# The middle tap of Hyena's short convolutions on ScalarE, and ScalarE's order in the attention piece by piece

## What is computed

```python
def centred_conv(u, w):
    k = w.shape[0]
    r = k // 2
    length = u.shape[1]
    up = jnp.pad(u, ((0, 0), (r, r), (0, 0)))
    out = up[:, 0:length] * w[0]
    for i in range(1, k):
        out = out + up[:, i:i + length] * w[i]
    return out

def hyena_branch(pp, conv_w, w1, b1, freq, w2, b2, w3, bias):
    ...
    u = centred_conv(pp[..., OFF_HY:OFF_FN], conv_w).astype(F32)
    parts = jnp.split(u, HY_ORDER + 1, axis=-1)
    ...

def diff_softmax(q, k, v, lam):
    s = jnp.einsum('bhqcd,bhkcd->bhcqk', q.astype(F32), k.astype(F32)) * (A_DQK ** -0.5)
    p = jax.nn.softmax(s, axis=-1)
    a = p[:, :, 0] - lam * p[:, :, 1]
    return jnp.einsum('bhqk,bhkv->bhqv', a, v.astype(F32))
```

## Time and profile before

| | |
|---|---|
| median of 3 runs | 2013.67 us (2009.11 to 2014.9) |
| the profiled execution's own time | 2014.24 us |
| its span in the profile | 2012.5 us |
| TensorE busy (matmul) | 1890.2 us, 94% |
| VectorE, ScalarE, GpSimd busy | 1142.8, 782.0, 603.4 us |
| TensorE's granted clock, mean | 0.978 of full speed |
| attention stage, layer 0 | about 409 to 560 us of the span, turns 442.6 to 551 |
| attention stage, layer 1 | about 1521 to 1606 us of the span, turns 1547 to 1600 |

### The profile page before, as it was taken

The page is one execution under the profiler, slowest core; times in us unless marked ns, Lnnn a source line. Parts: engine busy times, 40 slices in busy tenths (PEclk is TensorE's granted clock), DMA queues, the critical chain, the costliest instruction groups (busy, mean ns, idle before and its releaser), DMA issues.

```text
span 2012.5 us, 32086 instructions
## 1 busy us (share of the span) xinstructions
PE 1890.2 (94%) x11466; PEld 1540.3 (77%) x11466; DVE 1142.8 (57%) x2009; ACT 782.0 (39%) x1593; POOL 603.4 (30%) x537
## 2 busy tenths in 40 slices
PE   6999889989989999998999999999988899998999
PEld 2566667766658888876888888777776789998999
DVE  4745863766674333345443343359777665567575
ACT  2325531335524322333322232256534544445453
POOL 3333122552121212126220132443446431134020
PEclk8999889999999999999999999999999999999999
DMA  7344454346521323322323332222213235554554
GB/s 240 124 136 147 158 169 131 121 131 210 177 72 50 98 94 94 99 89 84 94 94 97 102 94 94 79 84 83 87 43 121 77 120 179 174 166 150 179 181 143
DMA packets 225007, 244.62 MB, mean 122 GB/s; under 512 B 11459, under 2 KB 213508, under 8 KB 223876
## 3 DMA queue, kind: packets, MB, share of 16 engines
q1 hardware_dynamic: 221168, 226.62, 36.2%
q10 hardware_dynamic: 3732, 16.60, 2.2%
HBM read 236.90 MB, written 6.29 MB: 121 GB/s over the span
## 4 chain that ended last, share of the span: by engine, by line
PE 68%; DVE 12%; issue 10%; POOL 4%; ACT 3%; DMA 3%; ACTq 0%; DVEq 0%; POOLq 0%; SPq 0%
PE psum L638 54%; PE psum L633 12%; DVE big L2449 3%; DMA raw<-in_w_ada_dram 2%; POOL whl L1496 2%; DVE big L2458 1%; POOL big L3385 1%; ACT big L1707 1%; ACT whl L1487 1%; POOL big L3256 1%; DVE rstd L2449 1%; ACT big L1704 1%; PE psum L746 1%; DVE big L2711 1%; DMA big<-in_hy_table_dram 0%
## 5 line engine op out<-in xcount | busy, mean ns | idle before, releaser
L638 PE MATMUL psum<-hhl,whl 128*128 128x512 f32 (+1 forms) x4416 | 829.8, 348 | 27.9 <-DVE hhl L2583 16.8
L638 PEld LDWEIGHTS psum<-hhl,whl 128*128 128x128 f32 x4416 | 702.1, 193 | 153.8 <-issue 42.7
L1487 ACT CAST whl<-raw 128x512 fp32r<-128x512 f32 x656 | 374.2, 618 | 859.7 <-PE psum L638 856.1
L1496 DVE TENSOR_TENSOR whl<-raw,whl 128x512 fp32r<-128x512 f32 x480 | 330.1, 729 | 484.3 <-ACT whl L1487 483.4
L638 PE MATMUL psum<-bigr,whl 128*128 128x512 f32 (+1 forms) x2688 | 469.9, 336 | 4.7 <-DVEq L3175 2.5
L638 PEld LDWEIGHTS psum<-bigr,whl 128*128 128x128 f32 x2688 | 414.4, 190 | 57.7 <-issue 4.7
L1496 POOL TENSOR_TENSOR whl<-raw,whl 128x512 fp32r<-128x512 f32 x176 | 235.1, 1357 | 455.9 <-ACT whl L1487 440.1
L633 PE MATMUL psum<-big 128*128 128x128 f32 (+8 forms) x1572 | 244.5, 330 | 22.3 <-DMA big<-in_hy_w_dram 5.0
L633 PEld LDWEIGHTS psum<-big 128*128 128x128 f32 (+4 forms) x1572 | 165.7, 179 | 81.8 <-issue 53.3
L638 PE MATMUL psum<-whl,hhl 128*128 128x512 f32 x672 | 165.3, 405 | 6.0 <-POOL whl L1496 4.7
L3385 POOL TENSOR_TENSOR big<-big,tmp 128x512 f32<-128x512 f32 (+1 forms) x64 | 64.5, 1020 | 339.2 <-DVE tmp L3172 338.2
(11 more groups left out here) (176 smaller groups left out, 1405.5 us busy)
## 6 DMA issues: line engine op xcount, KB each, us to landing
raw<-in_w_mlp_dram SPq DMA_DIRECT2D x128, 512.0 KB, 3.6
raw<-in_w_ada_dram SPq DMA_DIRECT2D x96, 512.0 KB, 5.2
raw<-in_w_in_dram SPq DMA_DIRECT2D x88, 512.0 KB, 3.7
raw<-in_w_gate_dram SPq DMA_DIRECT2D x64, 512.0 KB, 3.5
raw<-in_w_branch_dram SPq DMA_DIRECT2D x32, 512.0 KB, 3.5
raw<-in_w_o_dram SPq DMA_DIRECT2D x16, 512.0 KB, 3.5
hy_spectra<-big ACTq DMA_DIRECT2D x2, 2560.0 KB, 10.2
big<-hy_spectra ACTq DMA_DIRECT2D x2, 1280.0 KB, 5.6
```

Of the source, the lines that this page charges most:

```text
L638: m = nc.tensor.matmul(o_, a(p_), b(q_), start=first and i == 0, stop=last and i == 2, skip_group_check=shared)
L1487: nc.scalar.copy(whl[:, r, 0, ks], raw_of(n)[:, ks]).then_inc(S["hi_ready"], 1)
L1496: ins = eng.tensor_tensor(whl[:, r, 1, ks], raw_of(n)[:, ks], whl[:, r, 0, ks].bitcast(F32), ALU.subtract)
```

## The change

A semaphore `hy_begun` is added. ScalarE gets `hy_begin`: it waits for the block and for the turning of the block two before, and writes the block times the middle tap into `HYB["cb"]` as an Identity activation with a column of `cols` as scale; it does not wait for itself afterwards. `conv` leaves the multiply out for Hyena's blocks and waits for `hy_begun` instead, before its first addition; DeltaNet's keep it. `u_copies` goes away: for each piece of a slot ScalarE now does the cast, then for a whole block the u copy of the block two before and the begin of this one, before it comes to the next piece. TensorE's, GpSimd's and SP's programs are the same.

```diff
@@ -2199,13 +2199,11 @@
                     for s, kh, cb in slot:
                         if cb:
                             hi_ahead(act, hy_strip[li, s, kh])
-
-                def u_copies(slot):
-                    for s, kh, cb in slot:
-                        if kh and s:
-                            u_copy(li, 2 * s + cb - 2)
+                        if kh:
+                            if s:
+                                u_copy(li, 2 * s + cb - 2)
+                            hy_begin(li, 2 * s + cb)
                 hy_ahead(slots[0])
-                u_copies(slots[0])
...
                     hy_ahead(slots[1 + u])
-                    u_copies(slots[1 + u])
                     if li == 0:
                         mod_row(0, FIRST_MODS + u)
...
+            def hy_begin(li, blk):
+                act.wait_ge(unit_done, hy_mark[li, blk])
+                if blk >= 2:
+                    act.wait_ge(filled, fill_at["hyu", li, blk - 2] + 1)
+                tk = toks(li)
+                f(HYB["cb"][:, blk % 2, tk], unit_bank[hy_unit[li, blk] % UNITS][:, tk], ACT.Identity,
+                  scale=cols[:, li, 0, 76 + blk:77 + blk]).then_inc(S["hy_begun"], 1)
...
@@ -2628,7 +2633,10 @@
-                ts(d3, p3, w[1], None, MUL)
+                if key == "hy":
+                    dve.wait_ge(S["hy_begun"], 12 * li + blk + 1)
+                else:
+                    ts(d3, p3, w[1], None, MUL)
```

More of the change, by code:

```diff
@@ L379, in build @@
                  "gates_turned fn_odd mod_turned amp_ready inverse_ready "
-                 "g_split k_sums kr_ready scales_ready far_ready decay_ready A_ready dit_ready it_ready diag_copied solved u_cleared udiag_dve "
+                 "hy_begun g_split k_sums kr_ready scales_ready far_ready decay_ready A_ready dit_ready it_ready diag_copied solved u_cleared udiag_dve "
                  "udiag_act tdiag y64_ready m64_dve m64_act t64_dve t64_act y128_dve y128_act u_dve u_act").split()
```

## The result

| | before | changed |
|---|---|---|
| median | 2010.67 us (2002.4 to 2014.9, 7 runs) | 2019.12 us (2007.78 to 2022.78, 7 runs) |
| ratio to before | | 1.0045, interval 1.0026 to 1.0064 |
| profiled execution, its span | 2014.24 us, 2012.5 us | 2007.78 us, 2006.0 us |

The change makes the kernel slower, by 5 to 13 us of some 2011. The forecast was +3.1 us, which would have been hardly distinguishable from no change; the time lies in the range, on the far side of the 0.3% line. That it lies there is in part luck (see the account of the prediction).

The account below looks back on a forecast made before the run. TensorE, busy 94% of the span, was taken as the bound. Terms 1.9 - 0.5 + 0.4 + 0.2 + 0.45 + 0.6 gave +3.1 us on the 2013.67 us median: 2016.7 us, range 2010.5 to 2021.5.

Parts of the forecast that it names:

- the second rival: TensorE's clock falls more often as waits lengthen, four more falls at 1.5 us each: +8.5 us, 2022.2 us; chance 0.12.
- Slower by over 0.3%: Whole kernel: the outcome that it slows by more than 0.3%, about 6 us; chance 0.13.
- ScalarE's multiply at 0.69 and 0.47 us: Both attention stages: price of each moved multiply on ScalarE, 0.69 us for 512 columns, 0.47 for 256.
- The Trainium skill's rule: Give multiplies to VectorE, up to three times faster in bf16; at 0.23 us here, the sum would be some 2 us larger.
- Layer 0, +1.9 us: Layer 0's attention turns: additions start 0.91 us behind the u copy, delaying TensorE; terms -0.2, +0.7, +0.7, +0.7.
- Layer 1, the start, -0.5: Start of layer 1's stage: ScalarE's multiply is ready early, so TensorE's 3.78 us wait shrinks by 0.52 us.
- Turn 1, +0.4: Layer 1, turn 1: second block's additions 0.36 us later, reaching TensorE's transposes; scores gain about 1 us, given back whole.
- Turn 3, +0.2: Layer 1, turn 3: same order would add another 0.4 us, halved because a GpSimd operation holds up VectorE.
- Turn 7 and the values, +0.45: Layer 1, turn 7: u block 0.52 us earlier, but probability copies behind two multiplies delay products with v: +0.45 us.
- The clock, +0.6, bounds 0 to 1.4: Layer 1: wait after turn 1 grows to 2.4 us, lower TensorE clock behind it, between 0 and 1.4, taken +0.6 us.
- The first rival: Multiplies ready before VectorE needs them, four in layer 0 and six in layer 1: 6.3 us faster, 2007.4; chance 0.08.
- The third: Attention stages decoupled: weight-load waits and long products swallow layer 0's delays, rest cancels: 0 to +1 us, 2014; chance 0.25.

Follow-up runs that it names:

- 1: The changed kernel run once more, unaltered, for a second profile: 2018.13 us, ratio 1.0036 to the kernel before.
- 3: Against the changed kernel: the change kept in layer 0 only, layer 1 as before; 2014.98 us, ratio 1.0028 to the kernel before.
- 8: Against the changed kernel: multiplies stay on ScalarE, casts again ahead of copies and multiplies except in each layer's first piece; 2018.06 us, ratio 1.0044.
- 2: Against the changed kernel: only ScalarE's new piece-by-piece order kept, VectorE keeps its multiplies; 2011.44 us, ratio 1.0013 to the kernel before.
- 4: Against the changed kernel: order and multiplies changed in layer 1 only, layer 0 as before; 2014.99 us, ratio 1.0028 to the kernel before.
- 9: Against the changed kernel: new order everywhere, ScalarE multiplies only blocks 0 and 10 of layer 1, VectorE the other 22; 2010.42 us, ratio 1.0007.
- 10: The kernel before run once more, unaltered, for a second profile: 2006.82 us, ratio 0.9990.
- 11: Against the kernel before, layer 1 only: new order in the first piece, turn 3's and turn 7's; ScalarE multiplies blocks 0 and 10; 2010.15 us, ratio 1.0005.
- 5: Against the changed kernel: ScalarE multiplies each pair's first block ahead of the u copy, the second behind it; 2015.46 us, ratio 1.0027.
- 6: Against the changed kernel: ScalarE multiplies both blocks ahead of the u copy of their piece; 2017.23 us, ratio 1.0026.

## Why the prediction was right, and where its size was wrong

The direction and the mechanism held, the size did not, and that the time lies in the range is in part luck. The range was laid around 2013.67 us, the median of three runs; seven runs of the kernel before gave 2010.67. As differences the forecast was +3.1 us and the range -3.2 to +7.8; measured are +8.5 by the medians and +9.0 by the ratio, which is past that edge, and is what the second rival had (+8.5). Slower by over 0.3%, which is what came, had a chance of 0.13.

- **ScalarE's multiply at 0.69 and 0.47 us: right** (687 and 473 ns). The Trainium skill's rule ("ScalarE: Activation LUTs", Rules for kernel authors) would have made the sum some 2 us larger because VectorE would have been the much faster engine; the durations don't bear that out for this fp32 operand in PSUM. The miss has another source.
- **Layer 0, +1.9 us: right, a little small.** The addition starts 1.00 us behind the copy, not 0.91 (the gap ahead of the multiply is 0.18, not 0.11), and the three delays are 0.81, 0.81 and 0.70. Layer 0's stage takes 130.3 us on average with its multiplies on ScalarE (128.5, 132.1, 128.8, 131.9, from the change, 1, 3 and 8) and 127.2 without (128.2, 125.7, 127.6, 128.9, 127.3, 125.7, from before, 2, 4, 9, 10 and 11): +3.1, with single profiles scattering by 3 to 4 us on waits for loads (5 and 6, in other orders, had 127.9 and 129.7).
- **Layer 1, the start, -0.5: right** (3.78 to 3.26 us).
- **Turn 1, +0.4: too small.** The mechanism held, the scores went at once and the time was given back; but the wait grew to 2.76 us, not 2.4. From the scores of turn 2 to those of turn 3 it took 7.54 us, before 6.85: +0.7. The second profile has 8.01; 0.46 of that are the transposes behind the wait at the lower clock.
- **Turn 3, +0.2: too small.** I halved this term for a GpSimd operation behind which a delay would hide. It hid nothing: the step that runs beside it took 1.33 us, before 1.22. The timeline of the changed kernel has VectorE's addition of the second block standing 0.82 us for a multiply which is behind a cast, a copy and a multiply:

```profile
1558.70 0.69 DVE L3070 TENSOR_REDUCE small<-psum 128x1 f32<-128x512 f32 x1 [2.82 <-PE psum L633]
...
1564.19 0.47 ACT L1704 ACTIVATE big<-psum,cols 128x256 f32<-128x256 f32 x1 [0.17 <-ACT big L1707]
...
1564.80 0.48 DVE L2463 SCALAR_TENSOR_TENSOR big<-psum,cols,big 128x255 f32<-128x255 f32 x1 [0.82 <-ACT big L1704]
...
1566.07 0.69 DVE L3070 TENSOR_REDUCE small<-psum 128x1 f32<-128x512 f32 x1
...
1568.22 1.33 DVE L2463 SCALAR_TENSOR_TENSOR small<-small 128x1 f32<-128x1 f32 x1
```

  The same steps in the kernel before:

```profile
1565.72 0.69 DVE L3062 TENSOR_REDUCE small<-psum 128x1 f32<-128x512 f32 x1 [1.87 <-PE psum L633]
...
1572.57 0.69 DVE L3062 TENSOR_REDUCE small<-psum 128x1 f32<-128x512 f32 x1
...
1574.72 1.22 DVE L2458 SCALAR_TENSOR_TENSOR small<-small 128x1 f32<-128x1 f32 x1
```

  From the scores of turn 3 to those of turn 5 it took 14.91 us, before 12.87. Of these 2.04 us, 0.95 are the scores at the lower clock, for which VectorE's maxima wait; 0.52 the late addition (7.37 us between the two maxima, before 6.85); 0.11 the step beside GpSimd; and 0.46 the transposes behind the wait at the lower clock (1.12 us for 0.66). So being late cost 0.6 us and not 0.2; the other 1.4 belong to the clock.
- **Turn 7 and the values, +0.45: right in kind.** The last u block came 0.52 us earlier and the products with v waited 0.94 us; net +0.4 of idle time. That the products themselves then ran at 0.64 was not foreseen, but the kernel before does that too in one profile of two.
- **The clock, +0.6, bounds 0 to 1.4: the term that was mis-sized most.** A fall makes TensorE busy 1.2 to 1.6 us longer (12 matmuls in 2.92 instead of 1.70 us; the products with v in 5.18 to 5.44 instead of 3.81), and the changed kernel has two more of them than before in these three places. I had allowed for one, and half of it hidden. Not all of it comes through: the fall of the order alone cost nothing, while that behind turn 3 cost 1.5 us in the kernel before (from the scores of turn 5 to those of turn 6 10.06 us with it, 8.56 without). In the changed kernel it is 1.4 us between the scores of turns 3 and 5, 0.5 less than before in the turn after these (9.59 us for 10.06), and 1.4 in the products with v: 2.3 us more than before, where I had 0.6.
- **The rivals.** The second, that the clock falls more often, had chance 0.12, and from about three falls on it was to decide. Two more falls in layer 1 and longer waits gave its +8.5 us, with fewer falls than its four and more waiting. The first rival fell: the multiplies are ready early in two places of 24, and there the gain was used up by the products with v. The third fell too: layer 0's late copies reached TensorE.

Summed over profiles, layer 0 costs 3.1 us and layer 1 4.9 (73.8 on average in the change, 1 and 4, less 68.9 in before, 3 and 10), 8.0 together, or 1.0040; the comparisons say 1.0036 and 1.0045. The forecast's sum had 1.9 and 1.15. So of the 4.9 us that it lacked, 3.75 lie in layer 1, in the waits behind turns 1 and 3 and in the clock, and 1.2 in layer 0, where single profiles scatter by more than that. In the one profile of the change layer 1's stage grew by 3.85 us, of which 2.3 are the clock as told above and 1.55 being late (0.7 after turn 1, 0.6 after turn 3, 0.5 ahead of the products with v, less 0.25 at the start), where the sum had 0.6 and 0.55. As causes the two can't be parted so cleanly. Experiment 9 took 3.0 us more than the order alone from turn 1's scores on with no late addition in turns 1 to 6, by its third fall, by where the falls lay and by GpSimd; the change and layer 1 alone took only some 0.9 us more than that, the change again 2.5. No run took the falls away and left the waits, so whether a longer wait brings a fall or only meets one stays open.

## What to carry to other kernels

An operation that goes to the engine with more idle time gets that engine's queue as well. Ask not which engine does it faster but when the result is there: here it stood 0.8 us behind a copy, and doing it twice made it 1.5 us. Where the engine that bounds the kernel already waits for the chain, such a delay goes through whole, and a longer wait of TensorE may be paid twice, the second time in its clock: behind waits of 2.06 us and more after turn 1 the clock was lower in nine profiles of nine.

## What the runs showed that was not expected

- TensorE's clock: behind waits of 1.08 to 1.09 us after turn 1 it stayed at 1.00 in four profiles of four; behind 2.06 to 3.79 us there it fell in nine of nine. The last wait alone does not decide: behind the same 2.10 us after turn 3 the clock fell in one profile of before and not in the other, and the products with v ran at 1.00 or at 0.57 behind waits of the same length (0.58 and 1.24 us), in the second case in the two of these profiles where it had not fallen behind turn 3. The Trainium skill ("TensorE: Matmul & The Clock Gate", What's actually happening) says that the monitor behind the clock runs freely against the program, so that the place of a transition varies from run to run; the two profiles of the unaltered kernel agree.
- VectorE's small steps beside GpSimd's 128x512 operations took 0.70 and 1.72 us instead of 0.22 and 0.75 in experiment 9; the small one took 1.33 in the changed kernel and already 1.22 in the kernel before. The Trainium skill ("GPSIMD Engine Reference", Specifications) has GpSimd share an SBUF interface with VectorE's instructions of two SBUF inputs; both steps are scalar-tensor-tensor, and the rows agree: the maxima and the small step of one input beside the same operations took 0.69 and 0.21 us as ever. Not each step is held up: one of 0.22 us stood inside such a stretch in the order alone.
- The u copy of either block frees a bank that scores wait for: with 0.69 us put ahead of it, TensorE waited 0.67 us at turn 7.
